# Five bursts of a discarded TensorE product between the mixer and the expert stage of a hybrid MoE block

## What is computed

```python
def reference(x, ...):
    h = rmsnorm(x, g_mix)
    proj = h @ w_in
    ...
    merged = gate_a * branch_a + gate_b * branch_b
    x = x + merged @ w_o
    h2 = rmsnorm(x, g_ffn).reshape(b * s, d)
    shared = swiglu(h2, s_gate, s_up, s_down)
    routed = routed_experts(h2, w_router, router_bias, e_gate, e_up, e_down)
    x = x + (shared + routed).reshape(b, s, d)
    return rmsnorm(x, g_final)
```

## Time and profile before

| | us |
|---|---|
| median of 3 runs | 2687.1 |
| the profiled execution | 2685.86 |
| its span (first to last instruction) | 2684.2 |
| PE busy in it | 2607.4 |
| DVE / ACT / POOL busy | 1793.1 / 1231.2 / 1310.6 |

### The profile page before, as it was taken

One profiled execution on the slowest core, in us unless ns is written; L12 is line 12 of the kernel. 1 busy time (PEld: TensorE's weight loads), 2 busy tenths in 40 slices (PEclk: granted clock), 3 DMA queues, 4 the chain that ended last, 5 costly groups with the idle time before them and its releaser, 6 DMA issues.

```text
span 2684.2 us, 50981 instructions
## 1 busy us (share of the span) xinstructions
PE 2607.4 (97%) x11854; PEld 2151.5 (80%) x11855; DVE 1793.1 (67%) x2537; ACT 1231.2 (46%) x1742; POOL 1310.6 (49%) x1093
## 2 busy tenths in 40 slices
PE   7999999999999999939999999999999999999998
PEld 6888888888888888827888888888888888888887
DVE  4544556556555655657877877777877777777677
ACT  3233323232333233215666666666666666666532
POOL 3000002120122013367877887777877877777722
PEclk9999999999999999959999999999999999999999
DMA  8223432442343333438988988888988888888676
GB/s 319 95 94 102 149 102 88 140 157 94 98 136 121 123 110 109 153 123 242 284 251 257 296 271 242 242 244 257 279 260 247 266 231 244 239 236 254 188 245 215
DMA packets 170046, 523.52 MB, mean 195 GB/s; under 512 B 37722, under 2 KB 43532, under 8 KB 170000
## 3 DMA queue, kind: packets, MB, share of 16 engines
q1 hardware_dynamic: 96208, 345.46, 35.7%
q0 software_dynamic: 65584, 163.32, 25.6%
q10 hardware_dynamic: 8208, 14.16, 1.6%
HBM read 434.94 MB, written 119.18 MB: 206 GB/s over the span
## 4 chain that ended last, share of the span: by engine, by line
PE 53%; DMA 1%; DVE 1%; POOL 0%; issue 0%; DVEq 0%; ACT 0%; SPq 0%; POOLq 0%
PE ps_gu L1556 12%; PE ps_gu L1554 11%; PE ps_gu L1555 11%; PE ps_y L1556 6%; PE ps_y L1555 6%; PE ps_y L1554 6%; PE ps_h L1610 1%; POOL xs L1483 0%; DMA xs<-h_dram,gidx 0%; DMA out<-expert_raw 0%; DMA expert_raw<-acc_odd 0%; DVE xt L1768 0%; DVE expert_raw L1863 0%; POOL rstd L1532 0%; DVE xl L1779 0%
## 5 line engine op out<-in xcount | busy, mean ns | idle before, releaser
L1483 POOL DMA_INDIRECT xs<-h_dram,gidx x656 | 819.7, 1250 | 202.2 <-issue 199.1
L1554 PE MATMUL ps_gu<-expert_hi,xl 128*128 (+1 forms) x1392 | 542.8, 390 | 21.0 <-DVE xl L1779 18.8
L1763 DVE TENSOR_TENSOR expert_lo<-expert_raw,expert_hi 128x1024 f32 (+1 forms) x390 | 459.6, 1221 | 126.7 <-ACT expert_hi L1640 123.8
L1556 PE MATMUL ps_gu<-expert_hi,xh 128*128 (+1 forms) x1392 | 543.0, 390 | 0.0
L1555 PE MATMUL ps_gu<-expert_lo,xh 128*128 (+1 forms) x1392 | 542.4, 390 | 0.0
L961 DVE TENSOR_TENSOR ul<-raw,uh 128x1024 fp32r<-128x1024 f32 x186 | 227.9, 1225 | 405.5 <-ACT uh L780 401.5
L1640 ACT ACTIVATE expert_hi<-expert_raw 128x1024 f32 (+1 forms) x390 | 390.8, 1052 | 67.6 <-PEq L1614 34.4
L95 POOL TENSOR_SCALAR rstd<-mean 128x1 f32<-128x1 f32 x29 | 6.5, 224 | 849.5 <-ACT junk L799 849.2
L539 PE MATMUL ps_t<-hh,ul 128*128 128x512 f32 x1024 | 401.9, 393 | 3.1 <-DVE wgl L1202 3.1
L540 PE MATMUL ps_t<-hl,uh 128*128 128x512 f32 x1024 | 399.6, 390 | 0.0
L541 PE MATMUL ps_t<-hh,uh 128*128 128x512 f32 x1024 | 399.4, 390 | 0.0
(11 more groups left out here) (282 smaller groups left out, 3919.0 us busy)
## 6 DMA issues: line engine op xcount, KB each, us to landing
expert_raw<-experts SPq DMA_DIRECT2D x396, 512.0 KB, 6.4
raw<-units SPq DMA_DIRECT2D x190, 512.0 KB
xs<-h_dram,gidx POOLq DMA_INDIRECT x656
h_dram<-h ACTq DMA_DIRECT2D x17, 512.0 KB, 4.8
acc_odd<-h POOLq DMA_DIRECT2D x17, 512.0 KB, 14.9
acc<-x SPq DMA_DIRECT2D x4, 2048.0 KB, 8.1
expert_raw<-acc_odd SPq DMA_DIRECT2D x16, 512.0 KB, 6.2
expert_raw<-x POOLq DMA_DIRECT2D x14, 512.0 KB, 3.6
```

The source lines that it names most:

```text
L1483: nc.gpsimd.indirect_dma_start(xs[s][:, g * DQ:(g + 1) * DQ], None, h2_quarters, bass.IndirectOffsetOnAxis(ap=gidx[s][:, g:g + 1], axis=0) ...
L1554: nc.tensor.matmul(out_, sl, vh, start=first, stop=False)
L1556: return nc.tensor.matmul(out_, sh, vh, start=False, stop=last)
L1763: V.tensor_tensor(l_, raw[:, p, :], h_, ALU.subtract).then_inc(piece_ready, 1)
```

## The change

One helper repeats the product of `ml` and one block of `mh` into the bank `ps_a`, which nobody reads again. It is called four times in `route`: 15 times after the router of the last tile but one (behind a new wait for `x2_added`, which says that VectorE has read `ps_a` for the seventh half), 13 times after the router of the last tile, 16 times after the last `count`, and 52 times behind the table's products. In `mixture`, 45 fp32 products of the identity with itself go to `ps_y1`, between the wait for `ident_ready` and the increment of `down_done`.

```diff
+            def keep_busy(times):
+
+                for _ in range(times):
+                    nc.tensor.matmul(ps_a[:, :], mh[:, 0, 0:P], ml[:, 0, :], start=True, stop=True)
+
...
                 router(n + 2)
+                pe.wait_ge(x2_added, c * 8 + TT + 7)
+                keep_busy(15)
                 count(n + 2)
                 turn_y(n + 3)
                 router(n + 3)
+                keep_busy(13)
                 count(n + 3)
+                keep_busy(16)
...
                              ).then_inc(tab_d, 1)
 
+            keep_busy(52)
             pe.wait_ge(tok_float, 1)
...
             pe.wait_ge(ident_ready, 16)
+            for _ in range(45):
+                nc.tensor.matmul(ps_y[1][:, 0:P], ident[:, :], ident[:, :], start=True, stop=True)
             pe.sem_inc(down_done, 1)
             n = pairs(pe)
```

## The result

| | median us | lowest to highest | runs |
|---|---|---|---|
| before | 2688.95 | 2686.16 to 2691.53 | 12 |
| changed | 2693.9 | 2692.8 to 2696.34 | 12 |

The ratio is 1.0018, with a 95% interval of 1.0011 to 1.0026: the change costs about 5 us. The median lies in the stated range (2685 to 2695.5) and 1.9 us above the forecast of 2692. A second comparison on another occasion gave 1.0019 (1.0010 to 1.0028). The profiled execution took 2692.93 us, its span 2691.2. The runs of before shown ahead of the prediction were at the fast end of what that kernel does, so the 7.1 us between the two profiled executions overstate the change.

A forecast was written before the change was run, and what follows sets the result against it. The prediction took PE, dense from 1221 us, and the chain of waits before it as the bound; -1.7 from `route`, +10 held signal and -3.6 absorbed gave +4.7 us on 2687.1, so 2692 us, range 2685 to 2695.5.

The forecast's parts named there:

- The bound: Expert stage: PE dense from 1221 us, so any shift of that start shifts the end by the same amount.
- The gain of the four bursts: In `route`: bursts keep the clock up, so the spread ends 1.7 us sooner, from 0 to 2.7 us.
- rival 2: In `route`: clock falls anyway, transposes wait for the 52; gain 0, signal held 11.2 us; 2694.7 us; chance 0.15.
- Rival 3: All bursts: clock holds everywhere, also into the fifth; -2.7 and 8.1 us for the signal; +2.0, 2689.1 us; chance 0.10.
- The held signal: In `mixture`: the increment of `down_done` waits behind the 45 products, holding ScalarE 10 us, bounds 0 and 12.
- Rival 1: In `mixture`: the increment slips past the fifth burst, leaving only the gain in `route`; 2685.4 us; chance 0.15.
- The slack: Start of the expert stage: idle time before VectorE's first turn and POOL's DMAs closing up absorb 3.6 us.
- The fifth burst's return: At `gate_up(0)`: the fifth burst gives nothing back; at most 0.4 us could pass, and the clock falls again first.
- The sum: Whole kernel: -1.7 from `route`, +10 for the held signal, -3.6 absorbed; +4.7 us, 2692 us.
- an increment after 58 matmuls: In `mixture`: the queue of 64 counted in single loads and matmuls leaves 32 pairs; the sum then comes to 2690.4.

The follow-up runs named there:

- after_again: The changed kernel, word for word, run once more beside the kernel before: 2693.47 against 2687.77 us, ratio 1.0019.
- only_fifth: The kernel before plus only the 45 products ahead of the increment of `down_done`: 2697.69 against 2692.65 us, ratio 1.0022.
- fifth_20: The kernel before plus 20 fp32 identity products ahead of the increment of `down_done`: 2688.05 us in 1 run, no ratio.
- fifth_inc_first: The kernel before plus only the 45 products, with the increment of `down_done` ahead of them: ratio 0.9997.
- control: The kernel before with no edit, timed beside the kernel before: 2692.29 against 2692.65 us, ratio 1.0003.
- only_route_again: A repeat of the changed kernel without its fifth burst, the four bursts in `route` kept: ratio 0.9994 to the kernel before.
- fourth_22: The changed kernel without its fifth burst, the fourth cut from 52 to 22 products: ratio 1.0003 to the kernel before.
- first set: The first of three sets of experiments, each on its own chip: `control`, `only_fifth`, `only_route` and `inc_first`; ratios 1.0003, 1.0022, 1.0010 and 1.0026.
- only_route: The changed kernel without its fifth burst, the four bursts in `route` kept: ratio 1.0010 to the kernel before.
- inc_first: The changed kernel with the increment of `down_done` moved ahead of the 45 products, all five bursts kept: ratio 1.0026.

## Why the prediction held, step by step

**The bound.** That PE is dense from the first product behind the wait, and that all shifts of it pass to the end, holds to the matmul: 6497 in 1439 us before and after, and the span is 7.0 us longer for a stretch that starts 7.0 us later. No term of the forecast holds H: in `after_again` the stretch began with 3.4 us at half clock, which is 1.7 us more.

**The gain of the four bursts.** Forecast 1.7 us, from 0 to 2.7. R shrank by 0.5 us in the first profile of the change and by 1.6 in the second. The parts came as worked out. From the start of the transposes to the end of the spread it took 3.1 us instead of 5.1, the 2.0 us of the forecast. The scatters of the last tile follow those of the tile before with the queue's own 0.30 us, so the 1 us that `dest_ready` gained did not help further; counted from the router's start they began 0.4 us sooner (forecast 0.66). What ate the gain in the first profile was the end of the 52: they ran 13.56 us instead of 11.8, because the clock was at half until 1173, and the lists had been cast at 1181.56, 1.9 us before the transposes could start. That is rival 2's mechanism, which had 0.15; in `route` the first profile lies nearer to it than to the forecast. I had put it at up to 2.6 us. The clock did not hold through: it fell inside the router at 1153 and again at 1166. Rival 3 falls with that.

**The held signal.** Forecast 10 us, measured 9.5, 9.8 and 10.2. The lead of the sequencer was 17 matmuls in three profiles and 15 in one; I had 13 to 17. The 13 of the router at 1153.1 did not repeat in the bursts. The first part of the burst that ran at half clock lasted about 3 us in the first profile (1190.8 to between 1193 and 1194), where I took 4. My lower value for it, 3.1 us before the rise at 1186, left out the transposes at half clock from 1181.54; with them it would have been 4.7 us, as at 1210. Rival 1 falls. The Trainium skill, page "TensorE: Matmul & The Clock Gate", table at its head, gives a queue of 64 for TensorE; here 15 to 17 loads and as many matmuls were still outstanding, about half of it if each counts one. The measured number decides.

**The slack.** Forecast 3.6 us absorbed, measured 2.4 in the first profile and 2.7 in the second: 9.5 us of delay made M 7.1 longer, where I had 6.4. The 2.9 us at the first turn were absorbed as forecast. The term that was mis-sized is the rest, POOL's DMAs closing up. I had the fourth turn 14.0 us behind the first; it came 15.0 behind it, later even than the 14.6 before. POOL began block 2's gather 2.1 us behind the first turn, as worked out, but its four DMAs took 6.1 us and not 5.2, so the gather of block 3 behind them began 8.3 us behind the first turn and not 7.3:

```profile
1214.47 1.83 POOL L1493 DMA_INDIRECT xs<-h_dram,gidx  x1 [0.30 <-issue]
1216.60 1.00 POOL L1493 DMA_INDIRECT xs<-h_dram,gidx  x1 [0.30 <-issue]
```

The same DMA takes 1.83 us in `after_again` and 1.82 in `only_fifth` and `fifth_20`, against 1.00 in the kernel before. SP's load of expert 1 starts at 1202.77 in the changed kernel (six pieces, 6.0 us of issues), against 1193.24 before, and so stands nearer to this gather. I had named that as something that might come in rival 2; that it makes the DMA longer was not shown. VectorE's new wait of 2.70 us for block 2's rows, at 1218.12, is not on this path: the fourth turn still waited 0.39 us for block 3's rows.

**The fifth burst's return.** Forecast none; the clock had fallen by 1208, 4 us before `gate_up(0)` at 1211.98. `fifth_inc_first` shows none even where the burst ends in time. Its `gate_up(0)` starts 1.4 us behind the burst at full clock, its first matmul takes 0.50 us instead of 0.80, and M is 35.4, no shorter than 34.6: VectorE waits for block 3's rows, now 2.60 us instead of 0.38.

```profile
1206.91 0.50 PE L1554 MATMUL ps_gu<-expert_hi,xl 128*128 128x512 f32 x1 [1.43 <-DVE xl L1781]
...
1223.36 0.79 PE L1554 MATMUL ps_gu<-expert_hi,xl 128*128 x1 [4.74 <-DVE expert_lo L1765]
```

```profile
1218.44 1.25 DVE L1770 STREAM_TRANSPOSE xt<-xs 128x1024 f32<-128x1024 f32 x1 [2.60 <-DMA xs<-h_dram,gidx]
```

**The sum.** Forecast +4.7 us and 2692 us; measured +5.0 and +5.7 by the medians. By R and M of the profiles it is -0.5 and +7.1, so +6.6, in the first, and -1.6 and +7.1, so +5.5, in the second. Both lie above the forecast, because the gain of `route` was too high by 1.2 and 0.1 us and the growth of M too low by 0.7. Within M the delay was 0.5 us too long and the absorbed part 1.2 us too large, and these two work against each other. The medians come closer to the forecast than the first profile does, in part because the profiled execution of before is a short one (2685.86 us against a median of 2688.95 over 12 runs). So that the sum holds to half a microsecond is luck; that the held signal outweighs the clock's gain is not. Two side sums of the rivals are off: rival 3's -2.7 + 8.1 - 3.6 is +1.8 and not +2.0, and an increment after 58 matmuls, at 8.3 us, gives about 2690.1 and not 2690.4.

## What to carry to other kernels

Before work of any kind is put into an engine's idle time, look at what stands behind it in that engine's stream: an increment that has nothing to do with the work is held as soon as the work is longer than the sequencer's lead (here 15 to 17 matmuls), and other engines may hang on it. Put signals first, fillers after. A faster clock is worth only what the path behind the faster step lets through: of the 4.7 us that full clock could take off the turn, the router, the transposes and the spread (0.9 + 1.8 + 0.4 + 1.6), R shrank by 0.5 to 2.1 us in the four profiles with no late signal and a fourth burst of 42 or 52, and no median shows a gain clear of the noise. Behind the turn and the router GpSimd's queue sets the pace.

## What I had not expected of the hardware

**A product that ends early may cost its clock later.** In `fifth_inc_first` `gate_up(0)` and `gate_up(1)` ran at full clock and were done 1.7 us sooner (counted from the spread's end), while the dense stretch began 0.8 us later. So the idle time before that stretch grew to 4.74 us (2.25 before), and the clock fell as it began. Windows of that kernel, then of the kernel before:

```profile
1223.00:1229.00 6.00, 5.64 (x13) 0.50 0.90 307
```

```profile
1221.00:1227.00 6.00, 5.73 (x27) 1.00 0.92 323
```

13 matmuls instead of 27 in 6 us: about 3 us are given back where nothing hides them. The same fall, for half as long, is in the profiles of `control` (1224.3 to 1227.7, after an idle time of 2.51 us) and `after_again` (1227.4 to 1230.8, after 1.81 us), and as long as here in `only_route_again`, which has no fifth burst (1219.5 to 1226.4, before and within a stretch that follows 3.45 us of idle time). In `fourth_22` there is none after 3.19 us. So the fall does not need the fifth burst, and the idle time alone does not tell whether it comes; that the longer gap made it here is likely and was not shown.

**TensorE's signals can come late.** In the first set ScalarE's sigmoid of tile n+2 started at 1146.32, released 2.0 us after the last router matmul's end at 1144.3, in `control`, which has no burst:

```profile
1146.32 0.22 ACT L828 ACTIVATE sc<-bank 128x64 f32<-128x64 f32 x1 [1.71 <-remote]
```

In the first profile of before the same step followed at once. All four profiles of the first set have this delay: 2.0 us in `control` and `only_fifth`, 2.2 in `only_route`, 3.3 in `inc_first`. At the table's first product, 8.5 us in `only_route` and 3.6 in `inc_first` come on top, and nothing in the two without bursts in `route`. None of the other profiles has such a delay. What makes them is open, and so is whether the bursts make them longer. They explain much of R in the profiles of `only_route` and `inc_first`; that they also explain the times of these two (+2.7 and +7 us by the ratios) is likely for `only_route` from its repeat, and open for `inc_first`, which was not repeated.
